# Scaling the gated outputs of eight heads: broadcasts from diagonal tiles, in two batches

## The reference, cut to what matters

```python
o = o * lax.rsqrt(jnp.mean(o * o, axis=-1, keepdims=True) + NORM_EPS) * o_gain   # per head of 128
o = o * jax.nn.silu(g)
return o.reshape(bsz, seq, D_MODEL) @ w_out
```

## Time and profile before

| | us |
|---|---|
| three runs | 1642.91, 1645.42, 1646.74 |
| median of the three | 1645.42 |
| profiled execution, its own time | 1642.91 |
| its span, first to last instruction | 1640.9 |
| PE busy in the span | 1567.5 (96%) |
| DVE busy | 645.1 (39%) |
| ACT busy | 581.5 (35%) |
| mean granted clock of PE | 0.97 |

### The profile page before, as it was taken

How to read it: one execution, slowest core, us unless ns; L and a number is a source line. 1 busy time by engine, 2 the same in 40 slices (tenths; PEclk the granted TensorE clock), 3 DMA queues, 4 the chain that set the end, 5 groups by cost and what they waited for, 6 DMA issues and landing times.

```text
span 1640.9 us, 27922 instructions
## 1 busy us (share of the span) xinstructions
PE 1567.5 (96%) x12058; PEld 1278.4 (78%) x12058; DVE 645.1 (39%) x1103; ACT 581.5 (35%) x933; POOL 28.0 (2%) x47
## 2 busy tenths in 40 slices
PE   6899999999999988999999899989899999999997
PEld 4898899999999956999999868988655656556563
DVE  3657755334344533654455444653311111111110
ACT  2532244334334445544444645553121111212111
POOL 1000000000000001000000000001000000000000
PEclk8899999999998989999999879999999999999999
DMA  9568736988876611455553323624699999999992
GB/s 330 186 206 273 240 111 199 303 279 281 285 257 199 219 52 46 155 185 187 183 189 105 103 78 123 249 91 156 269 418 424 421 420 421 424 422 421 422 423 99
DMA packets 204313, 404.25 MB, mean 246 GB/s; under 512 B 5013, under 2 KB 172210, under 8 KB 196018
## 3 DMA queue, kind: packets, MB, share of 16 engines
q1 hardware_dynamic: 202176, 397.43, 66.3%
q0 software_dynamic: 1648, 5.18, 1.1%
q10 hardware_dynamic: 386, 0.11, 0.0%
HBM read 401.63 MB, written 1.07 MB: 245 GB/s over the span
## 4 chain that ended last, share of the span: by engine, by line
PE 92%; DVE 4%; ACT 2%; DMA 1%; issue 1%; SPq 0%; ACTq 0%; DVEq 0%
PE ps L1698 28%; PE ps L2193 13%; PE ps L1919 8%; PE ps L2215 7%; PE ps L1733 5%; PE ps L1711 4%; PE ps L2180 4%; PE ps L2225 4%; PE ps L1760 3%; PE ps L1744 2%; PE ps L1948 2%; PE ps L1855 2%; PE ps L1780 2%; PE ps L1790 1%; PE ps L1959 1%; DMA arena<-in_mod_w 1%
## 5 line engine op out<-in xcount | busy, mean ns | idle before, releaser
L1698 PE MATMUL ps<-u,wsplit 128*128 128x256 f32 x3912 | 482.5, 284 | 3.2 <-DVE wsplit L1102 1.8
L1698 PEld LDWEIGHTS ps<-u,wsplit 128*128 128x128 f32 x3912 | 474.5, 192 | 4.9 <-DVE wsplit L1102 2.2
L1102 DVE TENSOR_TENSOR wsplit<-arena,wsplit 128x1024 fp32r<-128x1024 f32 x258 | 312.8, 1222 | 352.7 <-ACT wsplit L717 349.6
L717 ACT ACTIVATE wsplit<-arena 128x1024 fp32r<-128x1024 f32 x258 | 268.8, 1055 | 257.3 <-PE ps L1698 108.9
L2193 PE MATMUL ps<-arena 128*64 128x256 f32 x1408 | 155.7, 379 | 0.8 <-DVE arena L1619 0.8
L1624 DVE TENSOR_TENSOR arena<-arena,ps 128x256 f32<-128x256 f32 x32 | 13.5, 421 | 358.7 <-ACT arena L1068 358.7
L2193 PEld LDWEIGHTS ps<-arena 128*64 128x64 f32 x1408 | 101.0, 137 | 60.6 <-issue 12.0
L1919 PE MATMUL ps<-hid,wsplit 128*128 128x256 f32 x1056 | 130.2, 283 | 0.0
L1919 PEld LDWEIGHTS ps<-hid,wsplit 128*128 128x128 f32 x1056 | 128.2, 192 | 0.0
L1074 ACT ACTIVATE arena<-ps 64x512 f32<-64x512 f32 x64 | 37.8, 591 | 154.0 <-PE ps L2215 153.2
L1733 PE MATMUL ps<-wsplit,u 128*128 128x256 f32 x672 | 84.6, 287 | 0.0
(11 more groups left out here) (328 smaller groups left out, 1369.4 us busy)
## 6 DMA issues: line engine op xcount, KB each, us to landing
arena<-in_w SPq DMA_DIRECT2D x66, 2048.0 KB, 17.4
late<-in_w SPq DMA_DIRECT2D x30, 2048.0 KB, 17.6
arena<-in_mod_w SPq DMA_DIRECT2D x48, 1024.0 KB, 7.4
arena<-in_ffn_w_in SPq DMA_DIRECT2D x44, 1024.0 KB, 5.4
arena<-in_ffn_w_out SPq DMA_DIRECT2D x22, 1024.0 KB, 6.4
arena<-in_a_w_in SPq DMA_DIRECT2D x16, 1024.0 KB, 8.2
arena<-in_kv_mod_w SPq DMA_DIRECT2D x8, 1024.0 KB, 6.5
arena<-in_kv_w SPq DMA_DIRECT2D x8, 1024.0 KB, 7.5
```

What stands on the lines that cost most here:

```text
L717: act.activation(piece_buf(p, 0), piece_src(p), ACT.Copy).then_inc(hi_done, 1)
L1102: dve.tensor_tensor(piece_buf(p, 1), piece_src(p), piece_buf(p, 0).bitcast(F32), ALU.subtract).then_inc(lo_done, 1)
L1698: mm = pe.matmul(o, w_[:, k, :], u[:, x_, k, :], start=first, stop=last)
```

## The change

Seven things differ at the end of the mixer:

- The blocks of step 1 go into banks 2 and 3, where the last round's products lie, so PE waits for the first `select` of round 7 and then for the second (`a_cp`, 29 and 30). To that end DVE now writes the remainders of the last `g7` pieces before `select(7)`, not after it.
- The call that loads the square root's table early is gone.
- ACT multiplies the outputs by the gain, in two instructions of four heads each, behind its squares. DVE no longer does it in line 1284.
- DVE makes 16 diagonal tiles: the identity times one column of `stat` each, in a ring of four tiles (`diag`).
- PE multiplies a matrix of ones with each tile, into banks 0 and 1, which hold four heads. Each product waits for its tile, and the fifth and later tiles wait for the product four before. The second four heads wait until DVE has read the first four.
- Gate product, scaling, rounding and remainder are done for four heads at a time, and DVE does the two batches one after the other, with both remainders at the end.
- `project("a_out", ...)` starts when both remainders are written, and all of its pieces go through `linear`.

`diag` takes the place of `weigh` in SBUF. `weigh`, which is used much later, becomes a part of it.

```diff
-            table_of(ACT.Sqrt)
             for b in range(2):
                 act.wait_ge(a_mm, 4 * 8 + b + 1)
                 act.activation(attA[:, 4 * b:4 * b + 4, 1, :],
-                               ps[:, b, :].rearrange("p (h t) -> p h t", h=4), ACT.Copy).then_inc(a_x, 1)
+                               ps[:, 2 + b, :].rearrange("p (h t) -> p h t", h=4), ACT.Copy).then_inc(a_x, 1)
...
+            for n in range(2):
+                act.activation(qA[:, 4 * n:4 * n + 4, :], acc[:, 4 * n:4 * n + 4, :], ACT.Copy,
+                               scale=vec("a_out_norm")).then_inc(a_og, 1)
             act.wait_ge(a_var, 1)
             act.activation(stat[:, 16:32], stat[:, 0:16], ACT.Sqrt).then_inc(a_std, 1)
-            for hh in range(HA):
-                act.wait_ge(a_g, hh + 1)
-                act.activation(u[:, 0, hh, :], sq[:, hh, :], ACT.Copy).then_inc(a_hi, 1)
+            for b in range(2):
+                act.wait_ge(a_g, b + 1)
+                act.activation(u[:, 0, 4 * b:4 * b + 4, :], sq[:, 4 * b:4 * b + 4, :], ACT.Copy).then_inc(a_hi, 1)
...
             for r in range(8):
-                if r < 7:
-                    for p in jobs[("v" if r < 4 else "g") + str(r)]:
-                        lo_upto(p["w"] + LOOKAHEAD)
+                for p in jobs[("v" if r < 4 else "g") + str(r)]:
+                    lo_upto(p["w"] + LOOKAHEAD)
                 select(r)
...
-            for p in jobs["g7"]:
-                lo_upto(p["w"] + LOOKAHEAD)
-            wait_out(dve, jobs["g7"][-1])
-            for n in range(4):
-                two = slice(2 * n, 2 * n + 2)
-                dve.wait_ge(a_sq, n + 1)
-                dve.scalar_tensor_tensor(out=qA[:, two, :], in0=acc[:, two, :], scalar=vec("a_out_norm"),
-                                         in1=gA[:, two, :], op0=ALU.mult, op1=ALU.mult).then_inc(a_t, 1)
             dve.wait_ge(a_ss, 1)
...
             dve.reciprocal(stat[:, 32:48], stat[:, 16:32]).then_inc(a_rs, 1)
-            dve.wait_ge(a_t, 4)
-            for n in range(HA + 2):
-                if n < HA:
-                    dve.wait_ge(a_bc, 2 * (n // 2) + 2)
-                    dve.tensor_tensor(sq[:, n, :], qA[:, n, :], acc[:, n, :], ALU.mult).then_inc(a_g, 1)
-                if n >= 2:
-                    dve.wait_ge(a_hi, n - 1)
-                    dve.tensor_tensor(u[:, 1, n - 2, :], sq[:, n - 2, :], u[:, 0, n - 2, :].bitcast(F32),
-                                      ALU.subtract).then_inc(a_lo, 1)
+            dve.wait_ge(a_rs, 1)
+            for n in range(16):
+                if n >= 4:
+                    dve.wait_ge(a_bc, n - 3)
+                else:
+                    dve.wait_ge(bc_done, 1)
+                dve.tensor_scalar(diag[:, n % 4, :], ident[:], stat[:, 32 + n:33 + n], None, ALU.mult)\
+                   .then_inc(a_diag, 1)
+                if n % 8 == 7:
+                    b = n // 8
+                    four = slice(4 * b, 4 * b + 4)
+                    dve.wait_ge(a_og, b + 1)
+                    wait_out(dve, jobs["g7"][-1])
+                    dve.tensor_tensor(qA[:, four, :], qA[:, four, :], gA[:, four, :], ALU.mult).then_inc(a_t, 1)
+                    dve.wait_ge(a_t, b + 1)
+                    dve.wait_ge(a_bc, n + 1)
+                    dve.tensor_tensor(sq[:, four, :], qA[:, four, :],
+                                      ps[:, 0:2, :].rearrange("p b (c t) -> p (b c) t", t=T), ALU.mult)\
+                       .then_inc(a_g, 1)
+            for b in range(2):
+                dve.wait_ge(a_hi, b + 1)
+                dve.tensor_tensor(u[:, 1, 4 * b:4 * b + 4, :], sq[:, 4 * b:4 * b + 4, :],
+                                  u[:, 0, 4 * b:4 * b + 4, :].bitcast(F32), ALU.subtract).then_inc(a_lo, 1)
...
             pe.wait_ge(a_dec, 16)
-            wait_out(pe, jobs["g7"][-1])
             for b in range(2):
+                pe.wait_ge(a_cp, 28 + b + 1)
                 for n in range(4):
-                    mm = pe.matmul(ps[:, b, P * n:P * (n + 1)], kd[:, 4 * b + n, 0:P], qd[:, 4 * b + n, P:T],
+                    mm = pe.matmul(ps[:, 2 + b, P * n:P * (n + 1)], kd[:, 4 * b + n, 0:P], qd[:, 4 * b + n, P:T],
                                    start=True, stop=True)
...
-            pe.wait_ge(a_rs, 1)
+            wait_out(pe, jobs["g7"][-1])
             for hh in range(HA):
-                pe.wait_ge(a_t, hh // 2 + 1)
+                if hh >= 4:
+                    pe.wait_ge(a_g, 1)
                 for b in range(TB):
-                    mm = pe.matmul(acc[:, hh, P * b:P * (b + 1)],
-                                   stat[:, 32 + 2 * hh + b:33 + 2 * hh + b].to_broadcast([P, P]), ident[:],
-                                   start=True, stop=True)
-                mm.then_inc(a_bc, 1)
-            project("a_out", "ffn0", (a_lo, 0), follows=jobs["gate0_0"])
+                    pe.wait_ge(a_diag, 2 * hh + b + 1)
+                    pe.matmul(lin[hh % 4 // 2][:, hh % 2, P * b:P * (b + 1)], ones[:], diag[:, (2 * hh + b) % 4, :],
+                              start=True, stop=True).then_inc(a_bc, 1)
+            pe.wait_ge(a_g, 2)
+            pe.wait_ge(a_lo, 2)
+            project("a_out", "ffn0", None, follows=jobs["gate0_0"])
```

More of the change, by code:

```diff
@@ L233, in two_blocks @@
         stat = sb("stat", [P, 64])
-        weigh = sb("weigh", [P, DC, 2])
+        diag = sb("diag", [P, 4, P])
         small = sb("small", [P, 3, 64])
@@ L380, in two_blocks @@
         a_var, a_std, a_rs = sem("a_var"), sem("a_std"), sem("a_rs")
+        a_diag = sem("a_diag")
         a_bc = sem("a_bc")
         a_t = sem("a_t")
+        a_og = sem("a_og")
         a_g = sem("a_g")
@@ L466, in two_blocks @@
         fin = sem("fin")
+        weigh = diag[:, 0, 0:2 * DC].rearrange("p (k n) -> p k n", n=2)
         b_rel = sem("b_rel")
@@ L642, in _ @@
             pool.memset(attA, 0.0).then_inc(a_init, 1)
-            pool.wait_ge(a_lo, HA)
+            pool.wait_ge(a_lo, 2)
             pool.dma_start(mem_tok, mem_2[0].rearrange("(b p) d -> p b d", p=P)).then_inc(ld_mem, 16)
@@ L1407, in new_gains @@
                                   vec2[:, VEC["norm_mix_2"]:VEC["norm_mix_2"] + DC], ALU.mult).then_inc(mod_done, 1)
+                dve.wait_ge(a_bc, 16)
                 final = vec2[:, VEC["final_norm"]:VEC["final_norm"] + DC]
```

## The result

The changed kernel takes 1661.6 us (median of four runs, 1660.62 to 1666.17) against 1646.08 for the kernel before. Three more executions took 1663.09, 1663.13 and 1667.42. The ratio on record is 1.0108, with a 95% interval of 1.0086 to 1.0131: slower by 14 to 22 us, 18 in the middle; the two medians alone differ by 15.5. The forecast was 10.9 and the direction was right, but the size was not: by the ratio, the 1645.42 of before becomes 1663.2, and the forecast was 1656.3 with 1662 as its high end. The profiled execution of the changed kernel is the one of 1663.13, with a span of 1660.7.

The account below looks back on a forecast made before the run. PE was taken to bound the kernel (busy 96% of the span, 92% of the chain). Terms 1.7 + 0.3 + 6.9 + 2.0 = 10.9 us on the median of 1645.42 gave 1656.3, range 1650 to 1662.

Parts of the forecast that it names:

- part 1: Chunk-pair products (line 1876) move to banks 2 and 3 and wait for the select's first copy: +1.7 us.
- second rival: PE's clock falls already in the longer wait ahead of line 1876, slowing products and outputs: 13.9 us in all, chance 0.22.
- Part 2: Gain moves to ACT and the root's table loads behind its copies, ending just after the mean: +0.3 us.
- Part 3: Broadcasts and scaling in two batches, then both remainders: 12.2 us from reciprocal to `a_out` against 5.3, +6.9 at half clock.
- Part 4: `a_out` starts on a PE that has been idle, so its first records run at a low clock: +2.0 us.
- The zero behind the mixer: From `a_out` on, the same sequence of work as before was expected, with no term for added time.
- The rival that the delay is made up: PE's stop lets the weight stream of the first feed-forward layer run ahead, giving 10.9 us back: 1645.4, chance 0.03.
- The rival that the clock holds: Broadcasts and `a_out` run at the full clock: 6.9 us in all, 1652.3, chance 0.20.
- the rival of the earlier fall: The clock drops in PE's 3.8 us wait ahead of line 1876: 13.9 us in all, 1659.3, chance 0.22.

Follow-up runs that it names:

- b1: The kernel before, unchanged, executed again for a second trace; one run of 1645.73 us.
- d2: The changed kernel with the early load of the root's table put back; 1669.80 us, one execution.
- c1: The changed kernel with no stop between the two broadcast batches, tiles 9 to 12 made ahead of the first scaling; 1665.69 us.
- c2: The changed kernel with remainders written head by head and the first two pieces of `a_out` taking heads as they come; 1657.51 us.
- c3: The changed kernel without diagonal tiles: broadcasts from the 16 columns by a product with the identity, still in two batches; 1656.44 us.
- d4: The kernel before with 16 diagonal tiles alone, in a ring of four, all else head by head as before; 1649.28 us.
- e1: The kernel before with 28 unread products (12.1 us of work) between the broadcasts and `a_out`; 1661.53 us, ratio 1.0101.
- e2: The kernel before with 32 unread products (13.8 us of work) between the broadcasts and `a_out`; 1661.75 us, ratio 1.0095.
- a1: The changed kernel as it is, executed again for times and a second trace; median 1665.81 us, ratio 1.0127.

## Why the prediction was wrong

Two steps failed: part 1 prices the wait alone and no clock, and what lies behind the mixer was put at nothing.

**Part 1, the wait: right in place, wrong in what it did.** The products started 1.85 later, forecast 1.7. The step that failed is the term "+1.7", which holds the clock at 1.00 up to the sums. Its ground is the sentence under the second rival, "before, 2.11 left the clock alone". The clock fell in the wait of 4.0 in all nine traces that had it unfilled. The products then took 1.7 longer and outputs with sums 1.9 to 2.2: 3.6 to 3.9, and the rival had 3. The 2.1 was followed by a fall in six of seven traces; one trace was no evidence that it isn't.

This is the miss against the trace that the forecast was made from. Against b1, which had lost its clock at the same place, the end of the mixer costs 11.3 to 12.1, close to the forecast of 10.9: there the fall that the forecast left out of the change is in the base too, and the two nearly cancel.

**Part 2, the table: right.** Forecast 0.3, measured 0.1 to 0.25 (d2). The load started at 221.47, ahead of the mean (222.31), and ended at 222.75.

**Part 3, the tail: the mechanism right, the term too small.** Forecast 12.2 from reciprocal to `a_out`, measured 13.2 to 13.4. The two batches, one after the other, and both remainders at the end are what costs (c1, c2); the tiles are not (c3, d4). A burst with its handover took 3.8 to 3.9 and not 3.4, the first tile and its handover 0.43 and not 0.25, and there are two of each. The same stretch against the trace of before is +7.9 to +8.1, forecast +6.9.

**Part 4, the start at a low clock: right within its bounds.** Forecast 2.0, measured 1.25 in the first trace and 2.6 in the next two.

**The zero behind the mixer: the second step that failed.** The prediction has "from there on the same sequence of work as before" and no term for it. The sequence is the same, the time is not: the later part was +3.4, +1.2 and +1.2 in the three traces, against 0 and -2.5 before, so 1.2 to 3.4 against one and 3.7 to 5.9 against the other. With that, b1's whole span is 17.0, 14.2 and 14.2 shorter than those of the changed kernel. The part needs no idle stretch for its steps (e1 and e2 add none, and by the ratios cost 4.5 and 1.8 more than their work) nor `weigh` (a1). The traces show that it comes in steps where the clock falls or holds; whether any delay of this size costs 2 to 4 us on average, or this is chance among few executions, stays open. The interval of e1, 13.8 to 19.3, lies above its 12.1 of work; that of e2, 12.5 to 18.8, holds its 13.8.

The sum, with the measured terms of the first trace: 1.85 + 1.7 + 2.2 + 0.25 + 8.1 + 1.25 = 15.3. Of the 4.4 that this exceeds the forecast, 3.9 is the clock in part 1, 1.2 the tail, 0.15 the wait, and 0.8 was forecast too much. The rest of the 19.8 by which the first two traces differ, 3.4 and 1.1, has no term in the prediction. The rival that the delay is made up was wrong: nothing came back in the feed-forward layer. The rival that the clock holds was wrong for every trace of the changed kernel; the rival of the earlier fall is what happened. The chances have a slip: slower adds up to 0.50 + 0.20 + 0.22 and half of 0.05, 0.945, and not 0.93.

## What to carry to other kernels

Splitting a chain that runs head by head into two big batches saves instructions and loses the overlap: here 5.3 us of tail became 13.3, while the replaced operation itself (a tile for a column) cost half a microsecond. Before pricing a stretch, look at a second execution of the kernel before: after a wait of 2 us the clock held in one and fell in the other, 4 us apart in that stretch, though the whole times were only 2.8 apart. And on a program with many short waits, a single time can't judge an edit of 5 us; the landmarks in the trace around the edit can.

## What was not expected of the hardware

The fall of the clock after a wait of 2.1 us in one execution and not in another of the same kernel (35.98 against 31.92 for the same work). A burst of eight fp32 products at 0.50 takes 3.77 whether each waits for a tile or not. And the steps behind the mixer: in 18 traces that I lined up, the part from the feed-forward layer to the last expert varied from -3.3 to +10.2 us, in steps that lie where the granted clock fell or held. The Trainium skill, "TensorE: Matmul & The Clock Gate", section "Why this matters for your kernels", warns of idle gaps between bursts of matmuls. The traces agree, and here the clock fell after one of 2.1 us in six of seven.
